# Down projections with both parts of their input in one product of 512 columns

## The reference

```
y = (silu(h @ w_gate) * (h @ w_up)) @ w_down                      # first block
y = (gelu(conv(h @ w_up_gate)) * conv(h @ w_up_value)) @ w_down   # second block
```

## Time and profile before

| | |
|---|---|
| time of three runs | 2766.66 us median (2764.95 to 2768.22) |
| the profiled execution | 2765.04 us |
| its span, first to last instruction | 2763.2 us |
| mean granted clock of TensorE | 0.978 |
| TensorE products | busy 2632.7 us |
| VectorE | busy 1706.2 us |
| ACT | busy 1221.0 us |
| mean HBM rate | 197 GB/s |

### The profile page before, as it was taken

How to read it: one execution, slowest core, us unless ns; L and a number is a source line. 1 busy time by engine, 2 the same in 40 slices (tenths; PEclk the granted TensorE clock), 3 DMA queues, 4 the chain that set the end, 5 groups by cost and what they waited for, 6 DMA issues and landing times.

```text
span 2763.2 us, 54384 instructions
## 1 busy us (share of the span) xinstructions
PE 2632.7 (95%) x21278; PEld 2505.5 (91%) x21278; DVE 1706.2 (62%) x2393; ACT 1221.0 (44%) x1645; POOL 48.3 (2%) x98
## 2 busy tenths in 40 slices
PE   5799999899999999997999989999899999999996
PEld 1588888899999999997998989999899999999996
DVE  1388864676666666665644655554676666666666
ACT  1343454544444444444544544444544444444444
POOL 0000000000000000000000000000000000000000
PEclk9899999999999999998999999999999999999998
DMA  9988768466666666664444445555455555555552
GB/s 387 384 310 297 262 214 275 152 228 198 198 198 197 197 198 197 197 198 129 138 144 141 134 146 182 182 182 172 133 184 183 183 183 183 182 184 182 183 183 93
DMA packets 137001, 545.18 MB, mean 197 GB/s; under 512 B 15057, under 2 KB 17361, under 8 KB 124497
## 3 DMA queue, kind: packets, MB, share of 16 engines
q1 hardware_dynamic: 127248, 474.08, 51.7%
q0 software_dynamic: 9216, 67.11, 7.0%
q10 hardware_dynamic: 448, 2.75, 0.3%
HBM read 541.78 MB, written 2.10 MB: 197 GB/s over the span
## 4 chain that ended last, share of the span: by engine, by line
PE 89%; DVE 4%; ACT 3%; DMA 2%; issue 1%; ACTq 0%; DVEq 0%; SPq 0%
PE bank L1521 20%; PE bank L1522 20%; PE bank L1523 20%; PE bank L1658 8%; PE bank L1660 8%; PE bank L1659 8%; PE bank L1557 2%; DMA ada_pre<-in_ada_w 2%; ACT w_hi L504 1%; PE bank L1598 1%; DVE w_lo L933 1%; DVE y L996 1%; PE bank L1616 1%; DMA bf<-in_f_bias 1%; DVE xt L1013 0%
## 5 line engine op out<-in xcount | busy, mean ns | idle before, releaser
L933 DVE TENSOR_TENSOR w_lo<-raw,w_hi 128x1024 fp32r<-128x1024 f32 x836 | 1013.0, 1224 | 740.4 <-ACT w_hi L504 739.7
L504 ACT ACTIVATE w_hi<-raw 128x1024 fp32r<-128x1024 f32 x836 | 873.3, 1056 | 945.8 <-PE bank L1523 541.6
L1521 PE MATMUL bank<-h_hi,w_hi 128*128 128x258 f32 (+2 forms) x4112 | 1170.1, 285 | 35.9 <-DVE h_lo L1002 28.7
L1522 PE MATMUL bank<-h_lo,w_hi 128*128 128x258 f32 (+2 forms) x4112 | 1169.6, 284 | 0.0
L1523 PE MATMUL bank<-h_hi,w_lo 128*128 128x258 f32 (+2 forms) x4112 | 1165.8, 284 | 0.0
L1521 PEld LDWEIGHTS bank<-h_hi,w_hi 128*128 128x128 f32 x4112 | 777.3, 189 | 52.9 <-DVE h_lo L1002 30.8
L1523 PEld LDWEIGHTS bank<-h_hi,w_lo 128*128 128x128 f32 x4112 | 779.0, 189 | 0.0
L1522 PEld LDWEIGHTS bank<-h_lo,w_hi 128*128 128x128 f32 x4112 | 778.8, 189 | 0.1
L1658 PE MATMUL bank<-hid_hi,w_hi 128*128 128x256 f32 x1408 | 399.8, 284 | 6.9 <-DVE hid_lo L1227 6.3
L1660 PE MATMUL bank<-hid_hi,w_lo 128*128 128x256 f32 x1408 | 399.4, 284 | 0.0
L1659 PE MATMUL bank<-hid_lo,w_hi 128*128 128x256 f32 x1408 | 399.3, 284 | 0.0
(11 more groups left out here) (215 smaller groups left out, 2468.7 us busy)
## 6 DMA issues: line engine op xcount, KB each, us to landing
raw<-in_w_in SPq DMA_DIRECT2D x208, 512.0 KB, 3.8
raw<-in_w_ffn_up SPq DMA_DIRECT2D x176, 512.0 KB, 3.6
ada_raw<-in_ada_w POOLq DMA_DIRECT2D x64, 1024.0 KB, 6.6
raw<-in_w_gate SPq DMA_DIRECT2D x88, 512.0 KB, 4.1
raw<-in_w_up SPq DMA_DIRECT2D x88, 512.0 KB, 4.3
raw<-in_w_down SPq DMA_DIRECT2D x88, 512.0 KB, 4.1
raw<-in_w_ffn_down SPq DMA_DIRECT2D x88, 512.0 KB, 4.4
ada_pre<-in_ada_w SPq DMA_DIRECT2D x32, 1024.0 KB, 8.6
```

The source lines that it names most:

```text
L504: act.activation(w_hi[:, slot], raw[:, slot], ACT.Copy).then_inc(hi_ready, 1)
L933: dve.tensor_tensor(w_lo[:, slot], raw[:, slot], fp(w_hi[:, slot]), ALU.subtract).then_inc(lo_ready, 1)
L1521: pe.matmul(dst, wh, x_hi(kt), start=first and k == 0, stop=False)
L1522: pe.matmul(dst, wh, x_lo(kt), start=False, stop=False)
```

## The change

`hid_hi` and `hid_lo` become two views of one tile `hid_parts`, in which the 256 columns of the high part and the 256 of the low part of a K tile lie side by side. A new `half_wide` uses a whole bank for each output tile: w_hi times both parts is one product of 512 columns, w_lo times the high part one of 256 columns that is summed into the bank's first half. The two halves of a bank are thus two parts of the same output, and VectorE adds both to y: first columns 0 to 255 of the two banks, then, when that add is over, columns 256 to 511. ACT in the last down waits for the second add. A half now takes a pair of banks in turn.

```diff
-        hid_hi = place("hid_hi", "r2", 12288, [128, 4, SEQ], f32r)
-        hid_lo = place("hid_lo", "r2", 16384, [128, 4, SEQ], f32r)
+        hid_parts = place("hid_parts", "r2", 12288, [128, 4, 2, SEQ], f32r)
+        hid_hi, hid_lo = hid_parts[:, :, 0], hid_parts[:, :, 1]
...
-                with loop(act, NCHUNK - 1, (halves, 24), (done, 24), (banks, 8), (hids, 4), (taps, n_taps)) as i:
+                with loop(act, NCHUNK - 1, (halves, 24), (done, 24), (banks, 12), (hids, 4), (taps, n_taps)) as i:
                     chunk(i + 1, gate)
-                    skip(8, 4)
+                    skip(8, 8)
                     chunk(i + 1, up)
...
-                    act.wait_ge(bank_free[banks.bank() + j % 2], banks.had[banks.pair].at(1, 2))
+                    act.wait_ge(bank_free[banks.close() + 1], banks.read)
                     pair_square(step, j, y[:, 2 * j:2 * j + 2, SB])
...
                     convert()
                     dve.wait_ge(half_used, done.next())
-                    b = banks.bank() + j % 2
-                    dve.tensor_tensor(y[:, 2 * j:2 * j + 2, SB], y[:, 2 * j:2 * j + 2, SB], both(b), ALU.add)\
-                       .then_inc(bank_free[b], 1)
+                    b = banks.close()
+                    for part in range(2):
+                        if part:
+                            dve.wait_ge(bank_free[b], banks.read)
+                        dve.tensor_tensor(y[:, 2 * j:2 * j + 2, SB], y[:, 2 * j:2 * j + 2, SB],
+                                          bank[:, b:b + 2, SEQ * part:SEQ * part + SEQ], ALU.add)\
+                           .then_inc(bank_free[b + part], 1)
...
+            def half_wide(x):
+
+                slot, b = halves.mod(RING), banks.bank()
+                pe.wait_ge(lo_ready, halves.at(1, RING + 1))
+                for o in range(2):
+                    pe.wait_ge(bank_free[b + o], banks.free())
+                for kt in range(4):
+                    for o in range(2):
+                        wh = w_hi[:, slot, kt, o * 128:o * 128 + 128]
+                        wl = w_lo[:, slot, kt, o * 128:o * 128 + 128]
+                        pe.matmul(bank[:, b + o, :], wh, x[:, kt].rearrange("p a n -> p (a n)"), start=kt == 0, stop=False,
+                                  skip_group_check=True)
+                        mm = pe.matmul(bank[:, b + o, 0:SEQ], wl, x[:, kt, 0], start=False, stop=kt == 3,
+                                       skip_group_check=True)
+                mm.then_inc(half_used, 1)
+                halves.next()
+                banks.close()
...
                     for j in range(8):
-                        half_one(banks.bank() + j % 2, lambda kt: hid_hi[:, kt], lambda kt: hid_lo[:, kt], range(4),
-                                 True, True, banks.free())
-                        if j % 2:
-                            banks.close()
+                        half_wide(hid_parts)
```

More of the change, by code:

```diff
@@ L1305, in ffn @@
                 n_zero = 1 if with_ada else 2
-                with loop(dve, NCHUNK - 1, (halves, 24), (done, 24), (banks, 8), (hids, 4), (taps, 2 * n_taps),
+                with loop(dve, NCHUNK - 1, (halves, 24), (done, 24), (banks, 12), (hids, 4), (taps, 2 * n_taps),
                           (nexts, 2 * n_taps), (gelus, n_taps), (made, 2 * n_taps), (gates, n_gates), (rows, with_ada),
@@ L1641, in _, with half_one @@
             used = [banks.had[b // 2].at(1, 1) for b in range(4)]
-            def half_one(b, x_hi, x_lo, kts, first, last, free=None):
+            def half_one(b, x_hi, x_lo, kts, first, last):
                 slot = halves.mod(RING)
                 pe.wait_ge(lo_ready, halves.at(1, RING + 1))
-                if free is not None:
-                    pe.wait_ge(bank_free[b], free)
-                elif first:
+                if first:
                     pe.wait_ge(bank_free[b], used[b])
@@ L1765, in ffn @@
                 chunk()
-                with loop(pe, NCHUNK - 1, (halves, 24), (banks, 8), (downs, 4)):
+                with loop(pe, NCHUNK - 1, (halves, 24), (banks, 12), (downs, 4)):
                     chunk()
```

## The result

The changed kernel takes 2793.06 us (median of 4 runs, 2792.30 to 2794.32), the kernel before beside it 2767.44 us (4 runs, 2764.95 to 2769.03). The ratio is 1.0094, with a 95% interval from 1.0078 to 1.0110: slower by 25.6 us. The forecast was 2774.9 us, 8.2 us slower, and its range ended at 2791.0. The direction holds, and the costs of the second add, the banks and the last downs nearly do; the gain of the merged product does not.

A forecast was written before the change was run, and what follows sets the result against it. TensorE, busy 95% of the span, was taken to bound the kernel. Loop downs of the two FFNs (-12.8, +8.2) and their last downs (+5.7, +7.1) summed to +8.2 us, forecast 2774.9 us, range 2766 to 2791.

The forecast's parts named there:

- the second add: VectorE, each half: two adds take 1.41 us, 0.72 more than one; with the conversion 2.47 of 2.72 us, so it keeps up.
- the banks: Half j+2 waits for half j's adds: free in the first FFN, 2.10 us lost per down in the second, +8.2 us net.
- the last downs: Last down of each FFN, a ring over VectorE and ACT: turns 0.72 us longer, +5.7 us first FFN, +7.1 us second.
- The pair of products: TensorE's downs: a wide and a narrow product cost 340 ns instead of 360, saving 20 ns per pair, 1.28 us per down.
- the last two bounds: Price of a pair: 346.7 ns with 13.3 ns fixed per product, or 333.3 if a long stream hides the weight load.
- its other two signs: Prediction wrong if the second FFN's gap before half 2 is missing, or the last downs' turns are not 0.72 us longer.
- The 213 ns at half clock: Six 256-column steps in 1.28 us, exactly 256/1.2: read as a weight load adding nothing under a stream that long.
- the 5.0 ns for 16 more columns: Products of 272 columns at 125.0 ns against 120.0 for 256, where columns alone would add 6.7 ns.
- The bound by a fixed cost: TensorE's pair: 13.3 ns fixed per product gives 346.7 ns, saving 13.3 per pair; the sum would be +15.8 us (2782.5).
- The rival with 352 ns or more: TensorE's pair costs 352 ns or more, the pitch growing with the columns: +22 to +31 us, 2789 to 2798; chance 0.10.
- the clock rival: TensorE's clock falls in the last down, halves 3 to 7 at half clock: end 4.6 us later, 2779; chance 0.08.
- The faster rivals: No wait at half 2 of the second FFN, 2762, chance 0.05; or wide products at 131 ns, 2732, chance 0.03.

The follow-up runs named there:

- Experiment 6: The changed kernel with VectorE's conversion moved behind the two adds in each down step: 2754.80 us, ratio 0.9958 to the kernel before.
- changed, ACT ahead: The changed kernel with ACT's weight conversion for the next step ahead of the square and scaling, in the last downs alone: 2770.77 us, ratio 1.0014.

## Why the prediction was wrong

**The pair of products** is the step that failed. "I take the middle of the last two bounds, 340 ns" was mis-sized: it measured 353.3, so 6.7 ns saved instead of 20. It is also what the prediction named as a sign of being wrong, a pair outside 333 to 347 ns; its other two signs stayed away. The prediction's own rule, 1.14 us for each nanosecond per pair, turns that into 8.2 + 1.14 x 13.3 = 23.4 us, against 25.0 in the downs of the profile and 25.6 in the runs. The two readings that drew me below 346.7 were both poor. The 213 ns at half clock say that nothing is added to the columns of 256 at half clock; at full clock the 13.3 ns stay, also with 512 columns (226.7). And the 5.0 ns for 16 more columns were taken for a slope. The series alone gives 26.7 ns for 64 columns (120.0 to 146.7), 6.7 for 16, so 125.0 was not a slope but the pace of that stream. The kernel before shows this too: between two downs of the first FFN stand 384 products of 258 columns, from 1036.00 to 1081.88, 119.5 ns each, less than the 120.0 of 256 columns in the down. The bound by a fixed cost was right for products alone. The remaining 6.6 ns are the slower of two paces, which no row of the kernel before shows; why the downs take the slower one stays open.

**The rival with 352 ns or more**, which got a chance of 0.10 and 2789 to 2798 us, is what came in number (353.3, 2793), but not its reason: the price does not grow in proportion to the columns.

**The second add** was right: 1.40 us for two (forecast 1.41), 2.45 to 2.46 us per turn with the conversion (2.47).

**The banks** were right in place and time: in the first FFN no wait, in the second the first product of half 2 at 7.52 us after the down's start, where 7.43 was forecast. Experiment 6 shows the cause, since another order of the same instructions removes it. The loss against the merged product's gain came out larger, because the gain was smaller.

**The last downs** were right in mechanism, and in size for the first FFN (+5.7). In the second it was +8.3 for 7.1: the clock rival came in part. Half 6 began at full clock and had half clock for 3.4 us; the first product of half 7 is 4.44 us behind its first instead of 2.83. Against that, half 0 was 0.6 us shorter than before, and its stretch at half clock was shorter too.

**The faster rivals** did not come. The Trainium skill (TensorE: Matmul & The Clock Gate, "Back-to-back issue gap") gives N/2.4 + 2.5 ns for an isolated product. The bf16 series agrees (215.8 measured), the fp32r series does not (226.7, 11 ns more). The 131 ns that the same section gives as the sustained rate for 512 columns came in no series here: 226.7 and 215.8.

## What to carry to other kernels

Before merging two products, price the stream of that type and width, alone and in the mix in which it will run. What the merge can save is only the fixed part of one product, here 13.3 ns at best and 6.7 in the kernel, and one more operation on the evicting engine (the one that empties the banks) easily costs more. When a change doubles the banks that a step holds, list how late the first eviction of each stage already is: lateness that cost nothing can become a stall. Here the first add stood about 3 us behind the end of its half, and each of ten downs lost 1.96 us. A stall or a ring over two in-order engines is often only an order. Moving one conversion behind the adds, and one ahead of a square, turned 25.6 us lost into 19 gained. But 12.5 of these 19 the kernel before gets from the second move alone, so compare a change with the best order of the kernel without it.

## What the runs showed of the hardware

- Products of type fp32r with a weight load each, in series of 96: N/2.4 + 13.3 ns from 256 to 512 columns, 111.5 ns with 128 and 192; bf16 with 512 columns 215.8 ns. VectorE and ACT at work beside them make no difference (227.0 for 226.7).
- Inside the kernel before, streams of nearly the same width lie up to about 2 ns below this line: 256 columns have 120.0 ns in the downs but 117.8 in another stage (95 steps from 335.72 to 346.91), 258 columns have 119.5, and 272 have 125.0.
- The same stream of instructions on the same operands settles into one of two paces, 346.7 or 353.3 ns per pair of 512 and 256 columns, and keeps it to the end of the series (twelve series of 32 or 48 pairs). In the whole kernel the pace changed behind a wait in three of ten downs (changed, ACT ahead). Series of only 512 or only 256 columns showed one pace each, 226.9 and 120.0.
- In the second FFN's last down of the changed kernel, TensorE ran one half per turn of 5.13 us, with no wait over 2.12 us between halves 2 and 7. Its granted clock fell to half twice, for 3.4 us each (mean of the 36.3 us: 0.86).
